# Rotating the second mixer and moving the column sums of the norms in a Trainium2 kernel of two transformer blocks

## Chip, cores and metric

The kernel runs on one core of one Trainium2 chip. The metric is the device time of one execution in microseconds (us); lower is better. A difference of about 0.2% is what a measurement of this kernel can tell from none.

## What is computed

Two transformer-like blocks in one launch, on a sequence of 512 tokens with width 1024, all in float32. Cut to what matters:

```python
# first block (depth 1)
x = x + 0.5 * swiglu(rmsnorm(x)) ;  x = x + mixer1(rmsnorm(x)) @ w_out ;  x = x + 0.5 * swiglu(rmsnorm(x))
# second block (depth 2): layer 0 has the even mixer, layer 1 the odd one
for layer in range(2):
    mix = even_or_odd_mixer(rms_norm(x, g[layer, 0]))
    x = x + rms_norm(mix, g[layer, 1])                 # a post-norm
    h = rms_norm(x, g[layer, 2])                       # a pre-norm
    x = x + rms_norm(conv_ffn(h), g[layer, 3])         # a post-norm

def even_mixer(h, w_in, w_out, w_sc, rel_bias):        # "the second mixer"
    gate_b, gate_c, xa, q, k, v = split(h @ w_in)      # six parts of 512 columns
    y_a = gate_b * causal_dwconv(gate_c * xa, w_sc)
    y_b = dilated_attention(q, k, v, rel_bias)         # 8 heads of 64
    return concat([y_a, y_b]) @ w_out
```

## The kernel before

**Layout.** Activations stand transposed, features on the 128 partitions and the 512 tokens in a row. `xT` holds the residual stream as 8 tiles of 128x512. A product that must be float32-exact enough is made of three passes on TensorE: every weight and every activation is split into a high part of type fp32r and the remainder (`wH`, `wL`, `H`, `L`), and `products` (L1853 on, its matmuls at L1860, L1861, L1862) adds H·wH, L·wH and H·wL. A **unit** is one 128-column slice of a weight matrix: 24 matmuls for 8 input tiles, or 33 for 11.

**Streams.** A `Stream` is one weight matrix. SyncE's queue loads a unit into a `raw` buffer (`load_unit`, L1842), ScalarE makes `wH` (`split_hi`, L1848), VectorE `wL` (`split_lo`, L1853), then TensorE multiplies. `wH`/`wL` are a ring of four slots, so a unit's split waits for the product that last used its slot. `st.bank` says which of the eight PSUM banks a unit is summed in.

**Order.** Every engine's instruction order is written out by hand; engines meet only at semaphores. The phases are: FFN 1, mixer 1, FFN 2, mixer 2 (stream IN2), its output projection (OUT2), conv-FFN 3 (GU3, DN3), mixer 3 (IN3, OUT3), conv-FFN 4 (GU4, DN4).

**Entry of a phase behind a post-norm** (there are three: `gu3`, `in3`, `gu4`; functions `proj_act`, `proj_dve`, `proj_pe`, `enter_act`, `enter_dve`, `first_products`, `ffn_pe`). The last tile of the projection is squared by ScalarE (L1909), VectorE adds it to the running sum `ssq` (L1917), and TensorE multiplies `ssq` with a matrix of 1/1024 (`column_sum`, L1889), which gives the mean on all partitions. ScalarE's `root` (L1922 Ln, L1924 Exp) makes `rstd`. Then for each of eight tiles VectorE scales (L1976), adds to `xT` (L1979) and makes the low part (L1934), and ScalarE makes the high part (L1929). In the same loop ScalarE squares the new tile (L1951) and VectorE adds it (L1970), for the pre-norm that follows. TensorE begins with `first_products`: for each tile as it becomes ready, its three matmuls for each of the first four units, 96 in all. After the seventh tile (`stat_after=6`) it makes the column sum of the pre-norm. The norm's factor is applied when the products are read from PSUM (L2097 in an FFN, L1331 in mixer 3), since it is per token.

**A conv-FFN** then goes, for each of its 22 feature tiles: gate product times `rstd` (VectorE L2097), convolution (ScalarE L2044, VectorE L2108 twice), Silu (L2048), times the up product (L2117), high part (L2052), low part (L2121). The splits of later units stand between these in the order of both engines.

**Mixer 2** (`conv_attention_mixer`) has four bodies p = 0 to 3, each with six units, in the order gate_b, gate_c, xa, q, k, v (j = 0 to 5), and two heads. Body p multiplies the units of p+1 and lets the attention of p run between them: scores (L971, `bank4`, `bank5`), softmax on VectorE and ScalarE, transposes of the probabilities (`pe_probT`, L981, all in `bank6`), their copy to SBUF (`act_probT`, L770), products with v (`pe_pv_pair`, L999, `bank7`). There are eight transposes s = 0 to 7 for each p, even s for one head and odd s for the other. The last body has no units left; there the first five of eight input tiles of the four first OUT2 units (`proj_start`, 15 matmuls each) stand between. Weights of body p+1 that share `bank0`, `bank1` wait for ScalarE's `evac` of the earlier unit.

**Mixer 3** begins with `first_products`, and its queue on SyncE waits for all eight low parts (`u_ready`) before it loads the mask `before` and then units (1,0) and on (L1134 to L1138).

The lines that set the transposes' waits are:

```python
    def pe_probT(pe, p, s):
        pe.wait_ge(M.scaled, 8 * p + (s + 1))
        if s == 0:
            pe.wait_ge(M.v_ev, p + 1)
        else:
            pe.wait_ge(M.p_ev, 8 * p + s)          # the copy of transpose s-1
```

Of the kernel before, what the change touches and what calls it, by code (L numbers as in the profile page):

```python
# [68 lines left out]
class Stream:  # L69
# [5 lines left out]
    def __init__(self, dram, bodies, per, K, early=False, extra=None, split=None, first=None):  # L75
# [5 lines left out]
        self.bank = {4: (0, 1, 2, 3), 5: (0, 1, 2, 3, 0), 6: (0, 1, 2, 3, 0, 1), 7: (0, 1, 2, 3, 0, 1, 2)}[per]  # L81
# [605 lines left out]
def conv_attention_mixer(k, st, t, site):  # L687
# [9 lines left out]
    FIRST_BANK = (5, 6, 7, 0, 1, 2)  # L697
    k.free("m2", site.scratch)
# [41 lines left out]
    def evac(act, u, j):  # L740
# [6 lines left out]
        if j == 0:  # L747
            wait(act, M.yc, u)
            act.activation(gb[:], src, ACT.Copy).then_inc(M.evac, 1)
        elif j in (1, 2):  # L750
            wait(act, M.cu, u)
            act.activation((gc, xa)[j - 1][:], src, ACT.Copy).then_inc(M.evac, 1)
        elif j in (3, 4):
            wait(act, M.scores, 8 * u)
            act.activation(qk[:, j - 3], src, ACT.Copy, scale=0.125 if j == 3 else 1.0).then_inc(M.evac, 1)
        else:
            wait(act, M.v_tr, u)
            act.activation(vT[:], src, ACT.Copy).then_inc(M.evac, 1)
# [7 lines left out]
    def act_probT(act, p, s):  # L766
        w = score_tile(s // 2)
        act.wait_ge(M.p_tr, 8 * p + (s + 1))
        wait(act, M.pv, 8 * p + (s - 1))
        act.activation(probT[:, s % 2, 0:w], bank[6][:, 0:w], ACT.Copy).then_inc(M.p_ev, 1)  # L770

    def act(act, after):
        def body(p, units, prev, tail):
            u = p + 1

            def slot(j):
                if units and not (isinstance(u, int) and u == 0 and j < st.early):
                    k.split_hi(act, st, u, j)
                if prev and not units and j < after.early:
                    k.split_hi(act, after, 0, j)  # L780
# [6 lines left out]
            if prev:  # L787
                evac(act, p, 3)
                evac(act, p, 4)
            slot(1)  # L790
            if prev:
                evac(act, p, 5)
# [12 lines left out]
            if units:  # L805
                evac(act, u, 0)
            slot(3)
            if prev:
                act.wait_ge(M.yc, p + 1)
                act.activation(k.tile_of(k.H, site.y + p), yc[:], ACT.Copy).then_inc(M.yc_hi, 1)  # L810
                act.wait_ge(M.v_tr, p + 1)
                act.activation(v_tok[:], bank[6][:].rearrange("p (a n) -> p a n", a=4), ACT.Copy).then_inc(M.v_ev, 1)
            if units:
                evac(act, u, 1)
            slot(4)
            if prev:
                act_probT(act, p, 0)
                act_probs(act, p, 2)
                act_probT(act, p, 1)
                act_probs(act, p, 3)  # L820
            if units:
                evac(act, u, 2)
            slot(5)
            if prev:
                act_probT(act, p, 2)
                act_probs(act, p, 4)
                act_probT(act, p, 3)
                act_probs(act, p, 5)
        k.split_hi(act, st, 0, 4)
        k.normal_act(act, site, 0, 4)  # L830
        k.split_hi(act, st, 0, 5)
        k.normal_act(act, site, 4, DT)
        act.wait_ge(M.tab_sum, 2)
        act.dma_start(t["dist_table"], table[0:8, :]).then_inc(M.tab_out, 16)
        act.wait_ge(M.tab_out, 16)
        load_params(act, 0)
        body(0, True, True, False)
# [29 lines left out]
    def dve_scaled(dve, j):  # L867
# [3 lines left out]
        dst, src, by = (gb[:], gc[:], xa[:], qk[:, 0], qk[:, 1], vT[:])[j], bank[FIRST_BANK[j]][:], k.rstd_mix[:]  # L871
        if j == 3:
# [3 lines left out]

    def dve(dve, after):
        def body(p, units, prev, tail):
            u = p + 1

            def slot(j):
# [1818 lines left out]
```

## Time and profile before

| | us |
|---|---|
| median of three runs | 2425.26 (2423.40 to 2427.48) |
| the profiled execution, its own time | 2428.54 |
| its span, first to last instruction | 2425.7 |
| TensorE matmuls busy | 2360.0 (97%) |
| VectorE busy | 1293.6 (53%) |
| ScalarE busy | 995.1 (41%) |
| GpSimd busy | 159.0 (7%) |
| mean granted TensorE clock | 0.989 |

The profile follows one execution. "Idle before" a row is time in which that engine did nothing ahead of it, with the instruction whose semaphore ended the wait. In a timeline the first column is the start in us from the span's start, the second the duration of the merged instructions; the end of a matmul is modelled, so distances are best taken from start to start.

### The profile page before, as it was taken

To read this page: it belongs to the slowest core of one execution; us is meant where nothing else is said; L and a number is where in the kernel's file an instruction comes from. 1 tells how busy PE (TensorE), PEld (TensorE's weight loads), DVE (VectorE), ACT (ScalarE), POOL (GpSimd) and SP (SyncE) were. 2 spreads that over 40 slices of the span, in tenths; PEclk is the share of its full clock that TensorE was granted. 3 is DMA by queue.
4 is the path that set the end of the run, shared out by engine and by line. 5 is a ranking of instruction groups with operands and counts; after the bars stand their busy time and mean duration, and the time that the engine had idled before them with its cause. 6 is when DMAs were issued, how large, how long until landed. Compare 5 with 4: busy or idle time off the path is not lost.

```text
span 2425.7 us, 30921 instructions
## 1 busy us (share of the span) xinstructions
PE 2360.0 (97%) x10918; PEld 1900.0 (78%) x10918; DVE 1293.6 (53%) x1832; ACT 995.1 (41%) x1481; POOL 159.0 (7%) x140
## 2 busy tenths in 40 slices
PE   8999999999999899999999989999989998999998
PEld 6888887777777688888877678888877766888887
DVE  5444436666655634433465475554258986655524
ACT  4222225756677422232234444333234454433322
POOL 0000002334333000000000000000000000000000
PEclk9999999999999999999999999999999998999999
DMA  4332322222322222232222122323213212232321
GB/s 163 97 99 100 106 91 93 83 100 73 99 73 84 79 94 95 95 106 96 93 90 96 61 71 94 101 91 120 95 35 106 77 63 70 81 101 95 118 96 47
DMA packets 62183, 219.91 MB, mean 91 GB/s; under 512 B 7664, under 2 KB 12272, under 8 KB 62112
## 3 DMA queue, kind: packets, MB, share of 16 engines
q1 hardware_dynamic: 60944, 216.86, 27.0%
q10 hardware_dynamic: 1168, 2.12, 0.3%
q8 instruction: 43, 0.70, 0.1%
q14 instruction: 28, 0.23, 0.0%
HBM read 216.83 MB, written 2.12 MB: 90 GB/s over the span
## 4 chain that ended last, share of the span: by engine, by line
PE 86%; DVE 5%; ACT 5%; issue 3%; DMA 0%; ACTq 0%; DVEq 0%; SPq 0%
PE bank L1860 26%; PE bank L1861 26%; PE bank L1862 26%; ACT m_prob L239 1%; DVE wL L1853 1%; PE bank L549 1%; ACT wH L1848 1%; DVE m_prob L358 1%; PE bank L592 0%; PE bank L971 0%; PE bank L999 0%; PE bank L981 0%; DVE m_mx L363 0%; PE bank L1559 0%; PE bank L2232 0%
## 5 line engine op out<-in xcount | busy, mean ns | idle before, releaser
L1860 PE MATMUL bank<-H,wH 128*128 128x512 f32 x3012 | 1194.4, 397 | 33.4 <-DVE L L1934 15.4
L1861 PE MATMUL bank<-L,wH 128*128 128x512 f32 x3012 | 1177.8, 391 | 0.0
L1862 PE MATMUL bank<-H,wL 128*128 128x512 f32 x3012 | 1177.8, 391 | 0.0
L1853 DVE TENSOR_TENSOR wL<-raw,wH 128x1024 fp32r<-128x1024 f32 (+1 forms) x361 | 470.9, 1311 | 611.9 <-ACT wH L1848 611.8
L1860 PEld LDWEIGHTS bank<-H,wH 128*128 128x128 f32 x3012 | 568.6, 189 | 166.2 <-issue 22.9
L1862 PEld LDWEIGHTS bank<-H,wL 128*128 128x128 f32 x3012 | 568.8, 189 | 120.6
L1861 PEld LDWEIGHTS bank<-L,wH 128*128 128x128 f32 x3012 | 569.2, 189 | 118.4 <-issue 3.8
L1848 ACT ACTIVATE wH<-raw 128x1024 fp32r<-128x1024 f32 (+1 forms) x361 | 396.5, 1106 | 213.2 <-PE bank L1862 204.6
L2052 ACT ACTIVATE H<-prod 128x512 f32 (+1 forms) x88 | 55.7, 633 | 243.5 <-DVE prod L2117 243.5
L2097 DVE TENSOR_TENSOR gate_s<-bank,rstd 128x512 f32<-128x512 f32 x88 | 60.8, 691 | 113.9 <-PE bank L1862 111.8
L2117 DVE TENSOR_TENSOR prod<-silu_g,bank 128x512 f32<-128x512 f32 x88 | 60.3, 685 | 79.7 <-PE bank L1862 73.6
L634 POOL TENSOR_TENSOR m_bias<-m_run,m_mask 128x256 f32<-128x256 f32 x64 | 77.2, 1244 | 382.8 <-DMA m_run<-in_rpb 382.8
L1929 ACT ACTIVATE H<-xT,cols 128x512 fp32r<-128x512 f32 (+1 forms) x56 | 39.9, 722 | 151.4 <-DVE xT L2379 120.6
L2041 ACT ACTIVATE silu_g<-gate_s 128x512 f32<-128x512 f32 x44 | 27.9, 633 | 162.0 <-DVE gate_s L2097 162.0
L2044 ACT ACTIVATE silu_g<-gate_s,cols 128x512 f32<-128x512 f32 x44 | 35.9, 815 | 114.5 <-DVE gate_s L2097 114.5
L2108 DVE SCALAR_TENSOR_TENSOR silu_g<-gate_s,cols,silu_g 128x511 f32<-128x511 f32 x88 | 66.1, 751 | 30.7 <-ACT silu_g L2044 25.1
L239 ACT ACTIVATE m_prob<-m_prob,m_mx 128x256 f32<-128x256 f32 x64 | 32.1, 502 | 72.5 <-DVE m_mx L363 72.5
L2121 DVE TENSOR_TENSOR L<-prod,H 128x512 f32 (+1 forms) x88 | 60.1, 683 | 3.0 <-ACT H L2052 2.8
L2048 ACT ACTIVATE silu_g<-silu_g 128x512 f32<-128x512 f32 x44 | 27.8, 632 | 76.8 <-DVE silu_g L2108 76.8
L1367 DVE SCALAR_TENSOR_TENSOR m_acc<-m_gp,cols,m_acc 128x512 f32<-128x512 f32 x84 | 57.5, 746 | 0.0
L1909 ACT ACTIVATE square<-mixT 128x512 f32<-128x512 f32 (+1 forms) x28 | 17.7, 632 | 96.8 <-DVE mixT L2370 51.2
L1934 DVE SCALAR_TENSOR_TENSOR L<-xT,cols,H 128x512 fp32r<-128x512 f32 (+1 forms) x56 | 41.2, 745 | 4.8 <-ACT H L1929 4.8
(267 smaller groups left out, 1670.6 us busy)
## 6 DMA issues: line engine op xcount, KB each, us to landing
raw<-in_w_ffn_gu SPq DMA_DIRECT2D x88, 512.0 KB, 3.4
raw<-in_w_in SPq DMA_DIRECT2D x56, 512.0 KB, 3.6
raw<-in_w_ffn_down SPq DMA_DIRECT2D x32, 704.0 KB, 4.1
raw<-in_w_up_2a SPq DMA_DIRECT2D x44, 512.0 KB, 3.4
raw<-in_w_up_2b SPq DMA_DIRECT2D x44, 512.0 KB, 3.4
raw<-in_w_in_even SPq DMA_DIRECT2D x24, 512.0 KB, 4.6
raw<-in_w_in_odd SPq DMA_DIRECT2D x24, 512.0 KB, 3.4
raw<-in_w_down_2a SPq DMA_DIRECT2D x16, 704.0 KB, 4.2
```

The source lines that it names most:

```text
L239: act.activation(prob[:, s % 2, 256 * b:256 * b + 256], prob[:, s % 2, 256 * b:256 * b + 256], ACT.Exp, bias=mx[:, e:e + 1], accum_out=den ...
L634: pool.tensor_tensor(bias[:, hh, n].rearrange("p (c r) -> p c r", r=ROWS), src, mask[:, MASK_OF[n]].rearrange("p (c r) -> p c r", r=ROWS), ...
L1367: dve.scalar_tensor_tensor(dst, src, w, dst, ALU.mult, ALU.add).then_inc(M.cv, 1)
L1848: act.activation(split_at(st, i, j)[0], raw_at(st, j), ACT.Copy).then_inc(S.hi_done, 1)
L1853: dve.tensor_tensor(w_l, raw_at(st, j), w_h.bitcast(F32), ALU.subtract).then_inc(S.lo_done, 1)
L1860: pe.matmul(out, w_h, xh[:, k0 + k], start=start and k == ks[0], stop=False)
L1861: pe.matmul(out, w_h, xl[:, k0 + k], start=False, stop=False)
L1862: last = pe.matmul(out, w_l, xh[:, k0 + k], start=False, stop=stop and k == ks[-1])
L2097: dve.tensor_tensor(gate_s[:, b], ffn_bank(i, 2 * b)[:], rstd[:], ALU.mult).then_inc(S.gate_ev, 1)
L2108: dve.scalar_tensor_tensor(silu_g[:, b, shift:], gate_s[:, b, 0:SEQ - shift], colr(w, (2 - shift) * FT + 2 * i + b), silu_g[:, b, shift:], ...
L2117: dve.tensor_tensor(prod[:, b], silu_g[:, b], ffn_bank(i, 2 * b + 1)[:], ALU.mult).then_inc(S.prod_done, 1)
L2121: dve.tensor_tensor(tile_of(L, ab + 2 * i + b), prod[:, b], tile_of(H, ab + 2 * i + b).bitcast(F32), ALU.subtract).then_inc(S.a_ready, 1)
```

## The change

It has three parts, which can be made one without the other.

1. **Mixer 2 is rotated.** The columns of its weights are reordered on the host to q, k, v, gate_b, gate_c, xa, and each body now multiplies gate_b, gate_c, xa of its own p and q, k, v of p+1. The last body therefore has three full units, and three of the four `proj_start` pieces; the fourth stands behind the last product with v. A piece covers six input tiles (18 matmuls). Units use three banks only, and the transposes of odd s go to `bank3`, so that a transpose waits for the copy of the one before the last. The convolution moves on VectorE behind scores 2 and 3. The table of distances is made right behind the first products.
2. **The last square of a post-norm** is no longer added by VectorE. TensorE multiplies `ssq` without it and the square itself into one bank (`post_sum`).
3. **The squares of the three pre-norms** stand behind all eight tiles and behind the splits of units (1,0) and (1,1). The column sum moves: in `gu3` and `gu4` behind unit (1,0), in `in3` behind the eighth tile.

```diff
+    T_BANK = (6, 3)
...
-        act.activation(probT[:, s % 2, 0:w], bank[6][:, 0:w], ACT.Copy).then_inc(M.p_ev, 1)
+        act.activation(probT[:, s % 2, 0:w], bank[T_BANK[s % 2]][:, 0:w], ACT.Copy).then_inc(M.p_ev, 1)
+
+    def unit_at(p, n):
+
+        return (p, n + 3) if n < 3 else (p + 1, n - 3)
...
-    early = (0, 1, 2, 4, 5)
+    early = (0, 1, 2, 4, 5, 6)
...
-        else:
-            pe.wait_ge(M.p_ev, 8 * p + s)
+        elif s > 1:
+            pe.wait_ge(M.p_ev, 8 * p + s - 1)
...
+        k.first_products(pe, c, site, [bank[b][:] for b in FIRST_BANK[:2]])
+        pe_table(pe)
+        dense(0, 2)
...
-    IN2 = Stream(t["w_in_even_2"], 4, 6, 8)
+    IN2 = Stream(t["w_in_even_2"], 4, 6, 8, banks=(0, 1, 2, 0, 1, 2))
...
-        gu3 = site(GU3, 0, 5, 32, gain(g2, 16), 4, 3, 6, rstd, post=gain(g2, 8), mix=0)
-        in3 = site(IN3, 0, 7, 40, gain(g2, 32), 4, 2, 6, rstd_mix, post=gain(g2, 24), mix=0, y=8,
-                   scratch=16)
-        gu4 = site(GU4, 22, 9, 48, gain(g2, 48), 4, 3, 6, rstd, post=gain(g2, 40), mix=22)
+        gu3 = site(GU3, 0, 5, 32, gain(g2, 16), 4, 3, None, rstd, post=gain(g2, 8), mix=0, squares_last=True)
+        in3 = site(IN3, 0, 7, 40, gain(g2, 32), 4, 2, 7, rstd_mix, post=gain(g2, 24), mix=0, y=8,
+                   scratch=16, squares_last=True)
+        gu4 = site(GU4, 22, 9, 48, gain(g2, 48), 4, 3, None, rstd, post=gain(g2, 40), mix=22, squares_last=True)
...
+        def post_sum(pe, c, on):
+
+            pe.wait_ge(S.ssq_done, adds(c.sums) + 7)
+            pe.matmul(bank[on][:], ones[:], ssq[:], start=True, stop=False)
+            c.sums += 1
+            pe.wait_ge(S.sq_done, 8 * c.sums)
+            pe.matmul(bank[on][:], ones[:], square[:, 1], start=False, stop=True).then_inc(S.stat_done, 1)
+            c.norms += 1
...
             for i, j in ((1, 0), (1, 1)):
                 split_hi(act, st, i, j)
+            for n in range(DT if site.squares_last else 0):
+                square2(n)
+            c.posts += 1
             root(act, c, site.stat_bank, site.rstd)
...
             for i, j in ((1, 0), (1, 1)):
                 split_lo(dve, st, i, j)
+            for n in range(1, DT if site.squares_last else 1):
+                add_square2(n)
+            c.posts += 1
...
                 unit_product(pe, st, 1, j, ffn_bank(1, j)[:], (H, L), site.u, True, True)
+                if j == 0 and site.squares_last:
+                    column_sum(pe, c, site.stat_bank, True)
...
-                add_square(dve, q, DT - 1, 1)
+                dve.wait_ge(S.sq_done, 8 * q + DT)
                 dve.tensor_copy(mixT[:, nxt.mix + DT - 1], bank[per - 1][:]).then_inc(S.proj_ev, 1)
```

Two places show the new order. The first is TensorE at the end of mixer 2's last body (`bank6`, `bank3` take transposed probabilities, `bank7` the products with v; the sizes are of the output). Before:

```order
L971 MATMUL bank4<-m2_qk_120 128x512 [waits m2_biased]
L971 MATMUL bank5<-m2_qk_120 128x512
L981 MATMUL bank6<-ident_58,m2_prob_122 128x128 [waits m2_p_ev,m2_scaled]
L981 MATMUL bank6<-ident_58,m2_prob_122 128x128 x2
L981 MATMUL bank6<-ident_58,m2_prob_122 128x128 [waits m2_p_ev,m2_scaled]
L981 MATMUL bank6<-ident_58,m2_prob_122 128x128 x3
L999 MATMUL bank7<-m2_probT_123,m2_v_tok_124 64x128 [waits m2_p_ev]
L999 MATMUL bank7<-m2_probT_123,m2_v_tok_124 64x128 x5
```

and in the change:

```order
L1871 MATMUL bank2<-H_50,wH_55 128x512
L1872 MATMUL bank2<-L_51,wH_55 128x512
L1873 MATMUL bank2<-H_50,wL_56 128x512
L990 MATMUL bank6<-ident_58,m2_prob_122 128x128 [waits m2_p_ev,m2_scaled]
L990 MATMUL bank6<-ident_58,m2_prob_122 128x128 x3
L1008 MATMUL bank7<-m2_probT_123,m2_v_tok_124 64x128 [waits m2_p_ev]
L1008 MATMUL bank7<-m2_probT_123,m2_v_tok_124 64x128 x5
L990 MATMUL bank3<-ident_58,m2_prob_122 128x128 [waits m2_p_ev,m2_scaled]
```

Before, transpose 6 follows transpose 5 and the last scores with nothing between; now 18 matmuls of an OUT2 unit stand ahead of it, and transpose 7 goes to another bank.

The second is VectorE in the entry `gu3`, from the last two tiles to the first gate. Before:

```order
L1976 SCALAR_TENSOR_TENSOR hf<-mixT,cols,rstd 128x512
L1979 TENSOR_TENSOR xT<-xT,hf 128x512
L1934 SCALAR_TENSOR_TENSOR L<-xT,cols,H 128x512
L1970 TENSOR_TENSOR ssq<-ssq,square 128x512
L1934 SCALAR_TENSOR_TENSOR L<-xT,cols,H 128x512
L1970 TENSOR_TENSOR ssq<-ssq,square 128x512
L1853 TENSOR_TENSOR wL<-raw,wH 128x1024 x2
L2097 TENSOR_TENSOR gate_s<-bank,rstd 128x512
```

and in the change:

```order
L2006 SCALAR_TENSOR_TENSOR hf<-mixT,cols,rstd 128x512
L2009 TENSOR_TENSOR xT<-xT,hf 128x512
L1958 SCALAR_TENSOR_TENSOR L<-xT,cols,H 128x512 x2
L1864 TENSOR_TENSOR wL<-raw,wH 128x1024 x2
L2000 TENSOR_TENSOR ssq<-square 128x512
L2000 TENSOR_TENSOR ssq<-ssq,square 128x512 x6
L2131 TENSOR_TENSOR gate_s<-bank,rstd 128x512
```

All seven additions of squares now stand between the splits and the first gate.

## Rows read from the trace of the kernel before

**Rows 1.** The page's first part: busy time, share and instructions of each engine.
```profile
PE 2360.0 (97%) x10918; PEld 1900.0 (78%) x10918; DVE 1293.6 (53%) x1832; ACT 995.1 (41%) x1481; POOL 159.0 (7%) x140
```
**Rows 2.** Waits of TensorE: who waited for whom, total us, times, longest us.
```profile
PE bank L1860 <- DVE L L1934: 15.4, 3, 5.2
...
PE bank L1889 <- DVE ssq L1917: 5.0, 3, 2.2
PE bank L981 <- ACT m_probT L770: 3.6, 4, 1.0
...
PE bank L981 <- DVE m_prob L864: 2.2, 1, 2.2
...
PE bank L999 <- ACT m_probT L770: 1.4, 2, 0.7
```
**Rows 3.** Timeline of TensorE in mixer 2: transposes and the last product with v.
```profile
1277.78 0.63 PE L981 MATMUL bank<-ident,m_prob 128*128 128x128 f32 x4 [0.97 <-ACT m_probT L770]
...
1388.95 0.97 PE L981 MATMUL bank<-ident,m_prob 128*128 128x128 f32 x4 [2.24 <-DVE m_prob L864]
...
1394.01 1.98 PE L999 MATMUL bank<-m_probT,m_v_tok 128*64 128x128 f32 x16 [0.69 <-ACT m_probT L770]
```
**Rows 4.** Busy time by stretch in mixer 2's last bodies; the column PEclk is the granted clock.
```profile
1362.00:1367.00 5.00, 3.48 (x41) 2.56 (x39) 4.20 (x7) 2.74 (x4) 0.00 (x0) 1.00 0.61 193
...
1392.00:1396.00 4.00, 3.08 (x21) 2.38 (x21) 0.00 (x0) 0.68 (x2) 0.00 (x0) 0.50 0.00 0
1396.00:1399.50 3.50, 3.50 (x9) 2.77 (x10) 1.39 (x2) 1.91 (x2) 0.00 (x0) 0.52 0.02 5
```
**Rows 5.** Timelines of VectorE and TensorE where OUT2's first units end.
```profile
1401.95 0.69 DVE L2372 COPY mixT<-bank 128x512 f32<-128x512 f32 x1 [1.37 <-PE bank L1862]
...
1404.29 1.23 DVE L1853 TENSOR_TENSOR wL<-raw,wH 128x1024 fp32r<-128x1024 f32 x1 [1.31 <-ACT wH L1848]
...
1405.83 0.40 PE L1860 MATMUL bank<-H,wH 128*128 128x512 f32 x1
```
**Rows 6.** Timelines of ScalarE and VectorE at the post-norm ahead of `gu3`.
```profile
1428.33 1.99 ACT L1848 ACTIVATE extraH<-raw 128x1024 fp32r<-128x1024 f32 x2
1430.38 0.69 ACT L1922 ACTIVATE rs<-bank,eps_col 128x512 f32<-128x512 f32 x1
...
1428.47 0.69 DVE L1917 TENSOR_TENSOR ssq<-ssq,square 128x512 f32<-128x512 f32 x1 [1.90 <-ACT square L1909]
...
1429.68 2.35 DVE L1853 TENSOR_TENSOR extraL<-raw,extraH 128x1024 fp32r<-128x1024 f32 x2
```
**Rows 7.** Timelines of TensorE and VectorE from `gu3`'s column sum to unit (2,1).
```profile
1456.99 1.02 PE L1889 MATMUL bank<-ssq,ones 128*128 128x512 f32 x2
1457.45 0.80 PE L1860 MATMUL bank<-H,wH 128*128 128x512 f32 x1
...
1459.44 0.69 DVE L2097 TENSOR_TENSOR gate_s<-bank,rstd 128x512 f32<-128x512 f32 x1 [4.51 <-PE bank L1862]
...
1465.59 1.23 DVE L1853 TENSOR_TENSOR wL<-raw,wH 128x1024 fp32r<-128x1024 f32 x1 [0.26 <-ACT wH L1848]
...
1484.95 1.23 DVE L1853 TENSOR_TENSOR wL<-raw,wH 128x1024 fp32r<-128x1024 f32 x1 [1.65 <-ACT wH L1848]
...
1487.82 0.39 PE L1860 MATMUL bank<-H,wH 128*128 128x512 f32 x1
```
**Rows 8.** Timelines of VectorE, SyncE's queue, ScalarE and TensorE in the entry `in3`.
```profile
1819.50 0.74 DVE L1976 SCALAR_TENSOR_TENSOR hf<-mixT,cols,rstd 128x512 f32<-128x512 f32 x1
...
1822.15 0.75 DVE L1934 SCALAR_TENSOR_TENSOR L<-xT,cols,H 128x512 fp32r<-128x512 f32 x1
1822.81 0.69 DVE L1970 TENSOR_TENSOR ssq<-ssq,square 128x512 f32<-128x512 f32 x1
...
1822.92 0.33 SPq L1135 DMA_DIRECT2D m_before<-in_before  x1
...
1827.41 2.26 ACT L1848 ACTIVATE wH<-raw 128x1024 fp32r<-128x1024 f32 x2 [5.17 <-DMA raw<-in_w_in_odd]
...
1828.80 0.80 PE L1860 MATMUL bank<-H,wH 128*128 128x512 f32 x1
```

More of the change, by code:

```diff
@@ L73, with __init__ @@
     newest = None
-    def __init__(self, dram, bodies, per, K, early=False, extra=None, split=None, first=None):
+    def __init__(self, dram, bodies, per, K, early=False, extra=None, split=None, first=None, banks=None):
         self.dram, self.bodies, self.per, self.K, self.extra = dram, bodies, per, K, extra
@@ L1007, in pe, with dense @@
     def pe(pe, c, after):
-        def body(p, units, prev, tail):
-            u = p + 1
-            def unit(j):
-                if not units:
-                    if prev and 1 <= j <= after.early:
-                        if j == 1:
-                            pe.wait_ge(M.evac, PER * N)
-                            for f in early:
-                                y_ready(pe)(f)
-                        k.proj_start(pe, after, j - 1, site.y, early)
+        def dense(i, j):
+            back = next(b for b in range(1, PER + 1) if st.bank[(j - b) % PER] == st.bank[j])
+            wait(pe, M.evac, PER * i + (j - back + 1))
+            if isinstance(i, int) and i == 0:
+                k.unit_product(pe, st, 0, j, bank[FIRST_BANK[j]][:], k.HL, site.u, True, True)
+            else:
+                k.unit_product(pe, st, i, j, bank[st.bank[j]][:], k.HL, site.v, True, True,
+                               v_ready(pe) if isinstance(i, int) and i == 1 and j == 0 else None)
@@ L1020, in unit @@
+        def body(p, units, prev, tail):
+            def unit(n):
+                if (n < 3 and prev) or (n >= 3 and units):
+                    dense(*unit_at(p, n))
                     return
-                if isinstance(u, int) and u == 0 and j < 2:
-                    if j == 0:
-                        k.first_products(pe, c, site, [bank[b][:] for b in FIRST_BANK[:2]])
+                if not (prev or n == 0):
                     return
-                back = next(b for b in range(1, PER + 1) if st.bank[(j - b) % PER] == st.bank[j])
@@ L1026, in unit @@
[L1026 to L1032 removed]
+                j = n - 3 if prev else 3
+                if j == 0:
+                    for f in early:
+                        y_ready(pe)(f)
@@ L1033, in body @@
+                if j < 3:
+                    pe.wait_ge(M.evac, PER * (N - 1) + (j + 4))
+                k.proj_start(pe, after, j, site.y, early)
+            if prev:
+                unit(0)
             if tail:
                 pe_pv_pair(pe, p - 1, 3)
+            if not prev:
+                unit(0)
             if prev:
```

230 lines of the change are left out of this document (112 added, 118 removed).

## The prediction

> **What bounds the kernel.** I read the busy shares first: TensorE is busy 97% of the span [rows 1], so only its idle time and its slow stretches can be won. The list of its waits says where that idle time is [rows 2]. Three kinds touch the change. At the three post-norms it waits 5.0 us for the last addition of squares, and then 15.4 us for the first low part of the new tiles. In mixer 2 it waits 3.6 + 1.4 us for copies of transposed probabilities and once 2.2 us for a scaled one, 7.2 us in all. The timeline puts the longest of these in the last body, where transpose 6 has nothing ahead of it [rows 3], and the stretches show what it brings: the granted clock is 0.50 from 1392 to 1396 and 0.52 until 1399.5, the lower of its two levels (1.2 of 2.4 GHz), whereas a similar stretch of transposes and small products 30 us earlier has 1.00 [rows 4]. All other terms are slack: how long before TensorE wants a unit its low part is there.
>
> **Scale.** From 1457.45 to 1487.82 TensorE starts 132 matmuls in a row [rows 7]: 12 of the last tile of the first products and five units of 24. One of them follows a column sum and takes 0.41 us longer, so a matmul is 0.227 us and a unit 5.45 us. The column sum costs 0.87 us (0.46 until the next matmul starts, and those 0.41).
>
> **Part 1, mixer 2.** All products stay; only waits go.
> - In the loop transpose 7 waited 0.97 us for the copy of transpose 6 [rows 3]. It now needs the copy of transpose 5, made one unit earlier: that wait goes in each body.
> - The last body had pieces of 15 matmuls and nothing at the sixth place. Now there are three full units and three pieces of 18 (4.1 us). In the rows of before, scaled probabilities 6 were ready 2.7 us after the last scores, so the 2.24 us wait [rows 3] is covered. Of the 7.2 us one wait of 0.69 us stays: the copy of transpose 7 ahead of the last product with v [rows 3].
> - Without the 2.24 us gap I expect the clock to stay up. What the low clock costs: half of 3.08 busy us in 1392 to 1396, 0.48 of the 3.5 us behind it [rows 4], and some 1.0 us for transpose 6 and its products before 1392 (the transpose took 0.97 us, its like in the loop 0.63 [rows 3]): 4.2 us.
> - A new wait: OUT2's first units are finished with two input tiles each instead of three, six matmuls fewer in units (0,2) and (0,3), 1.4 us. Behind the end of (0,1) come copy, square, high and low part of (1,0) in a chain that ends 3.57 us later (1401.95 to 1405.52) and was 0.3 us early for 1405.83 [rows 5]. TensorE now waits 1.1 us.
> - VectorE's queue has changed too: the convolution (3.6 us) stands ahead of a split and scores 4. By the durations of before, scaled probabilities 4 come 1.3 us before TensorE wants them in the loop and 0.3 us before in the last body. No wait, but thin.
>
> Sum: 7.2 + 4.2 - 0.7 - 1.1 = **9.6 us gained**.
>
> **Part 2, the last square.** TensorE no longer waits for a 0.69 us addition; its extra matmul on `ssq` runs while ScalarE squares. But ScalarE has two high parts to make, until 1430.32, before the Ln at 1430.38 [rows 6], so the root comes only 0.1 us earlier. VectorE makes two low parts until 1432.03 [rows 6] before it scales a tile; its copy starts 0.6 us earlier, but the first low part waits for the first high part (1429.38), so it gains 0.26 us. In `in3` its low parts already waited for the high ones: 0.1 us. Worth **0.6 us**, contained in the next terms.
>
> **Part 3, `gu3` and `gu4`.** Is the square in the tile loop on the path? VectorE needs 2.65 us a tile (1819.50 to 1822.15 [rows 8], the same in all three), TensorE 12 x 0.227 = 2.72 us, and its first tile runs at the low clock. So the loop already keeps up, and a faster VectorE starts nothing earlier. What moves is the column sum. Before, it starts at 1456.99 and the first gate at 1459.44 [rows 7], 2.45 us later. Now the first products end at 1460.6 - 0.87 - 0.26 = 1459.5, unit (1,0) at 1464.9, and the sum starts there: 7.9 us later. The first gate moves as much, and with it the chain gate, convolution, Silu, product, high part, split, in which each engine waits for the other and neither for TensorE. The low part of (1,2), done at 1466.82 [rows 7], is now done at 1474.7, and TensorE wants it at 1459.5 + 10.9 + 0.9 = 1471.2: a stall of 3.5 us. The slack is smallest at unit (2,1): low part 1486.18, wanted at 1487.82 [rows 7]. It is done at 1494.1 now: TensorE is **6.3 us late, in each of the two**. After that the steady loop is slower on TensorE than the chain, so the loss neither grows nor comes back.
>
> And the clock? A gap of 2.24 us once brought the low clock, and nine matmuls then filled 3.5 us [rows 3, 4], so the 3.5 us stall may do so too: some twelve matmuls of unit (1,2) 0.2 us longer each, 2.4 us. I add nothing for it, because the units behind wait for the chain: unit (2,0) then ends at 1493.5, still before 1494.1. The Trainium skill (TensorE: Matmul & The Clock Gate, section "HAM oscillation — how this bites in real kernels") warns that TensorE falls back to half rate in a long wait and starts the next burst cold; the rows agree that it does, and counted on top of the stalls, as that section counts it, it would make the sum 4.9 + 2 x 2.4 = +9.7 us.
>
> **Part 3, `in3`.** Without six additions of 0.6 us ahead of it the last low part is ready 3.6 us earlier, at 1819.3, so SyncE's queue, which waits for it (1822.92), issues its loads earlier and the high parts that waited 5.17 us for them start at 1823.8 instead of 1827.41 [rows 8] and end at 1826.1. The low parts end at 1827.3. Now the seven additions: the second waits for a square (1.35 us), five more follow at 0.72 us: 1832.9. TensorE ends the eighth tile at 1831.0, waits 1.9 us and makes the sum: unit (1,0) starts at 1833.8 instead of 1828.80 + 0.41 + 2.73 = 1831.9. **1.9 us lost.** `rstd_mix` comes 4.6 us later, but the low parts for the units behind have over 5 us of slack. The load that this hangs on is the uncertain one; between a load that lands as late as before (5.5 us lost) and additions hidden (0.9 gained) I take the moved landing.
>
> **Sum.** -9.6 + 6.3 + 6.3 + 1.9 = +4.9 us. The profiled execution took 2428.54 us, 3.3 above the median; from its own time this gives 2433.4, from the median 2425.26 **2430.2 us**, 0.2% more. A measurement of this kernel tells about 0.2% from no change (4.85 us), so the forecast is "slightly slower" and stands on the bound.
>
> **Rivals.**
> - *The late root is absorbed, and the kernel is faster.* For: VectorE is only 53% busy [rows 1], and the chain may close up where it had idle time. Against: the idle time ahead of the splits at 1465.59 and 1484.95 ends with ScalarE's high part [rows 7], which is in the chain itself. It decides if the chain can make up more than 7.9 - 1.6 = 6.3 us before unit (2,1). Then -9.6 + 1.9, and part 2's 0.6: 2417.
> - *The rotated body has its own waits.* The 1.3 us margin of scaled probabilities 4 is worked out from before; if splits bound to the unit just finished push it over, each body loses 1 to 2 us, or the tail keeps its low clock (4.2 us). Half the gain: 2435. Against: the 1.00 over a like stretch [rows 4].
> - *The clock adds to the stalls.* If the low clock lasts past unit (2,0) in `gu3` and `gu4`: 2 x 2.4 us more, 2435. For: a gap of 2.24 us was enough once [rows 3, 4].
> - *The chain is partly absorbed*, 3 us late instead of 6.3: 2424.
>
> **How the numbers follow.** The forecast gets 0.52, with its own range 2426 to 2434, half above the bound and half below. The absorbed root gets 0.17 (faster), the mixer's own waits 0.17 and the clock 0.08 (slower), the partly absorbed chain 0.06 (same). Slower 0.26 + 0.17 + 0.08 = 0.51, same 0.26 + 0.06 = 0.32, faster 0.17. The range takes in the first two rivals with the load's bound: 2416 to 2438.
>
> **What would show it.** In the profile after: new waits of TensorE for `wL` in units (1,2) and (2,1) of `gu3` and `gu4`, about 6.3 us in each; the first gate 7.9 us later behind the first products; in `in3` a wait for `ssq` of about 2 us at the column sum; in mixer 2 no wait ahead of transpose 7, one wait of 0.7 us at its end, the clock at 1.00 there, and about 1 us ahead of OUT2's unit (1,0); no wait of 1.4 us ahead of the sums at the post-norms, but still some 5 us behind each. Wrong, if TensorE has no wait for `wL` in the FFN entries, or if mixer 2 keeps its waits.

## The result: 7.3 us slower, and where the time went

The change takes 2433.66 us (median of 8 runs, 2431.60 to 2436.89), the kernel before 2426.37 us (8 runs beside them): ratio 1.0031, interval 1.0022 to 1.0040. That is slower by more than the 0.2% that a measurement tells, and inside the forecast range. The profiled execution took 2436.6 us, with a span of 2434.8 us (before 2425.7) and a mean granted clock of 0.987 (0.989). Two executions in the experiments took several times as long as all others of their kernels, 9371.79 us with the early loads alone and 7203.28 us with the filled gap, and are left out of the medians below.

The busy shares are what they were [rows 1]:

```profile
PE 2366.3 (97%) x10924; PEld 1900.7 (78%) x10924; DVE 1292.7 (53%) x1829; ACT 995.6 (41%) x1481; POOL 159.3 (7%) x140
```

The six matmuls more are those of the three `post_sum`, two records each. The waits of TensorE tell the story [rows 2]:

```profile
PE bank L1871 <- DVE wL L1864: 21.6, 10, 9.0
PE bank L1871 <- DVE L L1958: 17.0, 3, 5.7
PE bank L1913 <- DVE ssq L2000: 3.5, 1, 3.5
...
PE bank L1008 <- ACT m_probT L771: 0.7, 1, 0.7
PE bank L1902 <- ACT square L1933: 0.6, 1, 0.6
PE bank L990 <- DVE m_prob L871: 0.2, 1, 0.2
```

The 5.0 us for the last addition have become 0.6 us for a square, but the three waits for the first low part behind them have grown from 15.4 to 17.0 us. Of the 7.2 us in mixer 2 are left 0.7 + 0.2. New are 3.5 us for `ssq` and, from mixer 2 on, seven waits for `wL` of 9.7 us together. The kernel before has waits for `wL` too, but all of them ahead of mixer 2 (11.9 us, and 11.9 there in the change):

```profile
PE bank L1860 <- DVE wL L1853: 11.9, 4, 9.2
```

The spans compare like this (us, from the timelines of TensorE). The first row begins with IN2's column sum, each other row with the last product of the projection before it, so the wait for a post-norm's sum counts to the row behind it, and part 2 is contained in these rows:

| stretch | before | after | difference | forecast |
|---|---|---|---|---|
| IN2's sum to OUT2's last product (mixer 2) | 222.3 | 212.7 | -9.6 | -9.6 |
| to DN3's last product (`gu3`) | 370.3 | 377.3 | +7.0 | +6.3 |
| to OUT3's last product (`in3`, mixer 3) | 244.1 | 248.85 | +4.75 | +1.9 |
| to DN4's last product (`gu4`) | 364.1 | 370.4 | +6.3 | +6.3 |
| the end | | | +0.7 | 0 |

The sum, +9.1, is the difference of the two spans.

**Mixer 2.** TensorE at the last transpose and at the start of OUT2's unit (1,0), and the stretches that answer to [rows 4]:

```profile
1382.91 0.66 PE L990 MATMUL bank<-ident,m_prob 128*128 128x128 f32 x4
1384.26 1.09 PE L1008 MATMUL bank<-m_probT,m_v_tok 128*64 128x128 f32 x16 [0.69 <-ACT m_probT L771]
...
1396.12 0.47 PE L1871 MATMUL bank<-H,wH 128*128 128x512 f32 x1 [1.03 <-DVE wL L1864]
```

```profile
1392.00:1396.00 4.00, 3.09 (x14) 2.24 (x12) 2.28 (x4) 1.99 (x3) 0.00 (x0) 1.00 0.00 0
1396.00:1399.50 3.50, 3.38 (x15) 2.81 (x16) 2.45 (x4) 1.58 (x2) 0.00 (x0) 1.00 0.45 150
```

The kept wait of 0.69 us, the new one of 1.03 us ahead of (1,0), and a granted clock of 1.00 throughout: each as forecast.

**`gu3`.** TensorE from the column sum, then VectorE's first gate and the two splits that TensorE waits for [rows 7]:

```profile
1455.83 1.02 PE L1913 MATMUL bank<-ssq,ones 128*128 128x512 f32 x2
...
1461.95 0.39 PE L1873 MATMUL bank<-H,wL 128*128 128x512 f32 x1
1465.70 0.65 PE L1871 MATMUL bank<-H,wH 128*128 128x512 f32 x1 [3.36 <-DVE wL L1864]
1466.14 0.63 PE L1872 MATMUL bank<-L,wH 128*128 128x512 f32 x1
...
1485.05 0.50 PE L1871 MATMUL bank<-H,wH 128*128 128x512 f32 x1 [0.61 <-DVE wL L1864]
```

```profile
1458.28 0.69 DVE L2131 TENSOR_TENSOR gate_s<-bank,rstd 128x512 f32<-128x512 f32 x1 [10.96 <-ACT rstd L1948]
...
1464.42 1.23 DVE L1864 TENSOR_TENSOR wL<-raw,wH 128x1024 fp32r<-128x1024 f32 x1 [0.25 <-ACT wH L1859]
...
1483.77 1.23 DVE L1864 TENSOR_TENSOR wL<-raw,wH 128x1024 fp32r<-128x1024 f32 x1 [1.65 <-ACT wH L1859]
```

Counted from OUT2's last product, the sum has moved from 29.35 to 37.82 us, 8.5 us. The gate still comes 2.45 us behind it, and the low parts of (1,2) and (2,1) end 8.5 us later as well (39.2 to 47.6 and 58.5 to 67.0). The chain moves as one rigid piece. TensorE meets it at (1,2) with 3.36 us and at (2,1) with 0.61 us. Its slack can be read off: from the start of the sum to DN3's last product it is 340.9 us where TensorE does not meet the chain (before) and 339.4 where it does (after), so the slack was 1.5 us, and 8.5 - 1.5 = 7.0 us is what the stage lost. In `gu4` the sum moved by 7.8 us, and 7.8 - 1.5 = 6.3.

**`in3`.** VectorE, TensorE and SyncE's queue [rows 8]:

```profile
1822.20 2.60 DVE L1864 TENSOR_TENSOR wL<-raw,wH 128x1024 fp32r<-128x1024 f32 x2 [5.40 <-ACT wH L1859]
...
1826.11 4.67 DVE L2000 TENSOR_TENSOR ssq<-ssq,square 128x512 f32<-128x512 f32 x6 [0.70 <-ACT square L1974]
```

```profile
1826.96 0.39 PE L1873 MATMUL bank<-H,extraL 128*128 128x512 f32 x1
1830.83 1.83 PE L1913 MATMUL bank<-ssq,ones 128*128 128x512 f32 x2 [3.49 <-DVE ssq L2000]
1831.68 1.41 PE L1871 MATMUL bank<-H,wH 128*128 128x512 f32 x1
1832.89 0.63 PE L1872 MATMUL bank<-L,wH 128*128 128x512 f32 x1
```

```profile
1816.83 0.33 SPq L1146 DMA_DIRECT2D m_before<-in_before  x1
```

Counted from DN3's last product, the queue starts 3.5 us earlier (21.6 instead of 25.0 us behind it), as forecast. But the additions end 3.5 us behind the tile products, and behind that wait the two matmuls of the sum take 1.83 us instead of 1.02: the clock is low.

### The profile page after: what moved, and what is told of

It reads as the page before. It is cut to its first block, busy times and chain, and to the rows that moved or that the text cites. A ratio compares the mean times of both kernels' runs of the same rounds, so it can differ in the third digit from the quotient of the medians.

```text
span 2434.8 us, 30922 instructions
## 1 busy us (share of the span) xinstructions
PE 2366.3 (97%) x10924; PEld 1900.7 (78%) x10924; DVE 1292.7 (53%) x1829; ACT 995.6 (41%) x1481; POOL 159.3 (7%) x140
## 4 chain that ended last, share of the span: by engine, by line
PE 84%; DVE 7%; ACT 5%; issue 3%; DMA 0%; ACTq 0%; DVEq 0%; SPq 0%
PE bank L1871 26%; PE bank L1872 25%; PE bank L1873 25%; DVE wL L1864 1%; ACT wH L1859 1%; PE bank L549 1%; ACT m_prob L239 1%; DVE m_prob L358 1%; PE bank L592 0%; PE bank L1604 0%; PE bank L980 0%; PE bank L1008 0%; PE bank L1570 0%; PE bank L2266 0%; PE bank L2265 0%
## 5 line engine op out<-in xcount | busy, mean ns | idle before, releaser
L1871 PE MATMUL bank<-H,wH 128*128 128x512 f32 x3012 | 1196.7, 397 | 44.8 <-DVE wL L1864 21.6
```

The costliest lines, as they stand in the source:

```text
L1871: pe.matmul(out, w_h, xh[:, k0 + k], start=start and k == ks[0], stop=False)
```

## Experiments

All times are medians; each group ran beside its own runs of the kernel before. In these, the kernel before took 2427.57 us (12 runs, the first four), 2426.87 us (33 runs, the next four) and 2427.17 us (17 runs, the last four). It differs by 1.2 us from group to group, so a time set against one of another group is no surer than that.

### The parts alone

First part 1, and nothing else of the change:

```diff
-        gu3 = site(GU3, 0, 5, 32, gain(g2, 16), 4, 3, None, rstd, post=gain(g2, 8), mix=0, squares_last=True)
+        gu3 = site(GU3, 0, 5, 32, gain(g2, 16), 4, 3, 6, rstd, post=gain(g2, 8), mix=0)
...
-                post_sum(pe, c, 4)
+                column_sum(pe, c, 4, False)
...
```

> Part 1 alone. Theory (the three parts add up; mixer 2 gains 9.6 us by waits and low clock that go): 9.6 us under the kernel before, about 2416.8. In its trace mixer 2 has one wait of 0.7 us and one of 1.0 us ahead of OUT2's unit (1,0), and the granted clock stays at 1.00. Rival (what mixer 2 gains is partly given back in later stages, so the loss at the FFN entries is only the other side of it): under 5 us gained.

Measured: 2416.95 us, ratio 0.9955 (0.9942 to 0.9969). The mixer's 9.6 us are real and stand alone: the row of mixer 2 is 212.7 us here too.

Parts 1 and 2 (only the site lines go back):

> Parts 1 and 2, squares of the pre-norms in the tile loop as before. Theory: 0.6 us under part 1 alone (0.26 us at gu3 and gu4, 0.1 at in3), so 10.2 us under before, about 2416.2. A reader who prices part 2 by the addition it saves (3 x 0.7 us) expects 2.1 us under part 1 alone.

Measured: 2417.35 us, ratio 0.9947 (0.9934 to 0.9961). By these times part 2 can't be told from nothing. The five runs fall into two groups, 2411.39 and 2412.20 us at a mean granted clock of 0.995 and 2417.35 to 2417.96 us at 0.990, so the median of 2417.35 us, from which later expectations start, is that of the upper group. The traces do show part 2. In the waits it takes 4.4 us from the sums and gives 1.6 us back at the first low part, because that part was not waiting for the sum alone. What is left is the distance from OUT2's last product to the first product behind the post-norm, before and in the change:

```profile
1427.41 0.39 PE L1862 MATMUL bank<-H,wL 128*128 128x512 f32 x1
...
1435.52 0.80 PE L1860 MATMUL bank<-H,wH 128*128 128x512 f32 x1 [5.18 <-DVE L L1934]
```

```profile
1417.78 0.40 PE L1873 MATMUL bank<-H,wL 128*128 128x512 f32 x1
...
1425.64 0.80 PE L1871 MATMUL bank<-H,wH 128*128 128x512 f32 x1 [5.65 <-DVE L L1958]
```

It is 8.11 and 7.86 us; at `in3` it is 8.69 and 8.62, at `gu4` 8.12 and 7.87. That is 0.25 + 0.07 + 0.25 us, as expected. But at the kernel's end the wait for the last sum is 1.8 us in every version with part 2 and 1.4 us in every one without it, so 0.35 us go back there.

Part 3 on the kernel before (mixer 2 and the last square as before):

> Part 3 alone on the kernel before. Theory: +6.3 us in each of gu3 and gu4, and 4 to 4.7 us in in3 (as the trace of the change shows it): 16.6 to 17.5 us over before, about 2443.4. Rival (the loss needs the shorter mixer 2): 8 us or less over.

Measured: 2441.13 us, ratio 1.0055 (1.0041 to 1.0068), 13.6 us more, not 16.6. By stretches `gu3` is +6.5, `gu4` +6.0, but `in3` with mixer 3 only +1.3. Its wait for the squares is 2.38 us there instead of 3.49, because 12 slow matmuls ahead of it (7 in the change) made the tile products end later, and mixer 3 itself had fewer slow matmuls than in the profile of before. So what `in3` costs depends on where the clock is low. The same shows in mixer 2, which this version leaves as it was: with a gap of 2.25 us at the same place its row is 221.0 us instead of 222.3.

### Where the sum stands in the FFNs

The change with `stat_after=6` in `gu3` and `gu4`, squares still behind the tiles:

```diff
-        gu3 = site(GU3, 0, 5, 32, gain(g2, 16), 4, 3, None, rstd, post=gain(g2, 8), mix=0, squares_last=True)
+        gu3 = site(GU3, 0, 5, 32, gain(g2, 16), 4, 3, 6, rstd, post=gain(g2, 8), mix=0, squares_last=True)
...
-                if j == 0 and site.squares_last:
-                    column_sum(pe, c, site.stat_bank, True)
```

> The change, but gu3 and gu4 make the column sum after the seventh tile again (stat_after=6); the squares stay behind the tiles and the splits. Theory (the place of the sum on TensorE is what costs, since the additions end at about the time the seventh tile is multiplied): 12 us under the change, about 2421.7, with a wait for ssq of under 0.5 us at the sum. Rival (the late squares on VectorE and ScalarE cost, wherever the sum stands): no more than 3 us under the change.

Measured: 2421.66 us, ratio 0.9977 (0.9966 to 0.9987): the 12 us come back. Its waits of TensorE:

```profile
PE bank L1871 <- DVE wL L1864: 13.1, 4, 9.2
PE bank L1913 <- DVE ssq L2000: 5.1, 2, 4.1
```

All stalls at (1,2) and (2,1) are gone: from mixer 2 on, only the wait of 1.03 us ahead of OUT2's (1,0) is left. Of the waits for `ssq`, 4.1 us are `in3`'s, and 0.92 us stand ahead of the sum of `gu4`, more than the 0.5 us expected; in `gu3`, where 13 matmuls were slow behind the post-norm and not 6, there is none. The stage `gu3` takes 370.6 us from sum to sum, with the squares in the loop (parts 1 and 2) 369.8, and that difference of 0.8 is four slow matmuls (13 against 9). In `gu4` it is 364.3 against 364.0 us, with four slow matmuls fewer (6 against 10), which make up for most of the wait of 0.92 us. So taking the squares out of the tile loop brought nothing, and nearly all of the cost was the late sum. One tile later:

```diff
-        gu3 = site(GU3, 0, 5, 32, gain(g2, 16), 4, 3, 6, rstd, post=gain(g2, 8), mix=0, squares_last=True)
+        gu3 = site(GU3, 0, 5, 32, gain(g2, 16), 4, 3, 7, rstd, post=gain(g2, 8), mix=0, squares_last=True)
...
```

> The change, but with the column sum of gu3 and gu4 behind the eighth tile's products instead of behind the first unit's high products (before: behind the seventh). Theory (the lateness of the sum is what costs, and only what exceeds the slack of the chain of low parts): the sum stands one tile later than in the version with seven tiles, some 2.5 us later than before and 5 us earlier than in the change, so of the 3.4 us stall at (1,2) at most 0.8 us is left in each stage: 0 to 1.6 us over the version with seven tiles (2421.7), 2422 to 2423.5. Rival (it is the square behind the tiles, not the place of the sum, that costs): the sum itself then waits for the squares, and the time stays within 2 us of the change, 2432 to 2435.

Measured: 2423.36 us, ratio 0.9990 (0.9981 to 0.9999). One wait of 0.6 us in each of the two stages, at (2,1): `gu3` +1.3 us and `gu4` +0.8 over the version with seven tiles. In `gu3` the sum stands 2.7 us later than with seven tiles, so 1.5 us were slack, the same as above. The slack of the chain ends where the forecast put it.

### The entry of mixer 3

`in3` as before in the otherwise unchanged change:

```diff
-        in3 = site(IN3, 0, 7, 40, gain(g2, 32), 4, 2, 7, rstd_mix, post=gain(g2, 24), mix=0, y=8,
-                   scratch=16, squares_last=True)
+        in3 = site(IN3, 0, 7, 40, gain(g2, 32), 4, 2, 6, rstd_mix, post=gain(g2, 24), mix=0, y=8,
+                   scratch=16)
```

> The change, but the post-norm of in3 as before: squares among the tiles, sum behind the seventh tile. Theory (the sum of in3 waits for its additions, 3.5 us, and its clock falls behind that wait): the stage takes back the 4.75 us that it lost, 2433.7 - 4.7 = 2429.0 us, range 2428 to 2430. Rival (what the trace shows lost in in3 is shifted from the stages beside it and comes back there as another wait): 2432 to 2434.

Measured: 2428.42 us, ratio 1.0014 (1.0005 to 1.0023), 5.2 under the change by medians and 4.1 by the ratios (expected 4.7). The stretch takes 244.1 us instead of 248.85.

Or the loads earlier, with the squares behind the tiles:

```diff
+        for j in range(2):
+            k.load_unit(sp, st, 1, j)
         sp.wait_ge(S.u_ready, site.u0 + DT)
         sp.dma_start(before[:], t["before"]).then_inc(M.mask_loaded, 16)
...
```

> The change, but SyncE issues in3's first two loads of the second unit before it waits for the scaled tiles of the stage, so that the units' high parts on ScalarE are not held and the squares behind them come earlier. Theory (the squares of in3 stand behind a high part that waited for its load, which is why the additions end 3.5 us behind the tiles' products): the wait for the squares goes or falls under 0.5 us, and with it the slow stretch: 2433.7 - 4.5 = 2429.2 us, range 2428 to 2431. Rival (the additions are set by their own pace of 0.80 us a tile behind the last tile, not by the load): the wait stays over 3 us and the time stays at 2433 to 2434.5.

Measured: 2427.54 us, ratio 1.0010 (1.0001 to 1.0019), 6.1 under the change by medians and 5.1 by the ratios. VectorE and TensorE of this version:

```profile
1817.99 4.67 DVE L2004 TENSOR_TENSOR ssq<-ssq,square 128x512 f32<-128x512 f32 x6 [0.70 <-ACT square L1978]
```

```profile
1825.14 0.40 PE L1877 MATMUL bank<-H,extraL 128*128 128x512 f32 x1
1825.37 1.02 PE L1917 MATMUL bank<-ssq,ones 128*128 128x512 f32 x2
```

The additions take the same 4.67 us, but they end 2.7 us ahead of the sum: no wait, no slow matmul behind it. What cost `in3` its time was the load. The stretch from DN3's last product up to the sum of `m_ln_sum` in mixer 3 is 4.5 us shorter than in the change, as expected; another 2.5 us come behind it, where the change's profile has slow matmuls and this one has none, and that was not forecast.

The same version shows what the clock does to a stall. At `gu3`'s (1,2) it waits as long as the change, but stays fast behind it:

```profile
1463.03 0.50 PE L1875 MATMUL bank<-H,wH 128*128 128x512 f32 x1 [3.36 <-DVE wL L1868]
1463.36 0.40 PE L1876 MATMUL bank<-L,wH 128*128 128x512 f32 x1
...
1476.01 0.50 PE L1875 MATMUL bank<-H,wH 128*128 128x512 f32 x1 [1.47 <-DVE wL L1868]
```

The change had 7 slow matmuls there (some 1.4 us) and then no wait at the next unit; here there are none, and 1.47 us of wait come instead. Both reach (2,1) with 0.6 us to wait, and unit (2,1) starts 29.2 us behind the sum in both. Four profiles have the sum of `gu3` behind unit (1,0), with 0, 7, 13 and 13 slow matmuls behind the stall (this version, the change, part 3 alone, `in3` as before); from the sum to DN3's last product they take 339.46, 339.44, 339.47 and 339.43 us. Behind this rigid chain the low clock costs nothing.

### What in mixer 2 brings the gain

Parts 1 and 2, but all transposes in one bank:

```diff
-    T_BANK = (6, 3)
+    T_BANK = (6, 6)
...
-        elif s > 1:
-            pe.wait_ge(M.p_ev, 8 * p + s - 1)
+        else:
+            pe.wait_ge(M.p_ev, 8 * p + s)
```

> The change's second mixer and its last square by TensorE, squares of the post-norms as before (2417.35), but the transposes of both heads in one bank, with the wait for the other head's copy as before. Theory (the bank takes away the waits ahead of the second head's transposes, some 1 us each in three of the bodies, while the new order fills what waits elsewhere): 2417.35 + 3 = 2420.3 us, range 2419 to 2422. Rival A (the new order alone, not the bank, brings the gain of 9.6 us): within 1 us of 2417.35. Rival B (the bank is all of it, order nothing): 2424 to 2427.

Measured: 2422.63 us, ratio 0.9984 (0.9975 to 0.9993): 5.3 over parts 1 and 2, outside what each theory expected. Its row of waits, and one of them:

```profile
PE bank L990 <- ACT m_probT L771: 6.4, 8, 1.1
```

```profile
1305.17 0.63 PE L990 MATMUL bank<-ident,m_prob 128*128 128x128 f32 x4 [0.83 <-ACT m_probT L771]
```

There are two waits in each of four bodies, not one in three: ahead of transpose 7 (0.83 us) in all, ahead of transpose 1 (0.66 us) in the first three and of transpose 5 (1.13 us) in the last. The kernel before has the same pair of scores ahead of transposes 1 and 5 and no wait there. What is new is on ScalarE: a high part stands ahead of the copy. In the first body, with TensorE's transposes around it:

```profile
1236.65 0.27 PE L990 MATMUL bank<-ident,m_prob 128*128 128x128 f32 x1
...
1238.22 0.30 PE L990 MATMUL bank<-ident,m_prob 128*128 128x128 f32 x1 [0.66 <-ACT m_probT L771]
```

```profile
1236.85 1.06 ACT L1859 ACTIVATE wH<-raw 128x1024 fp32r<-128x1024 f32 x1 [4.36 <-PE bank L1873]
1237.81 0.26 ACT L771 ACTIVATE m_probT<-bank 128x128 f32<-128x128 f32 x1
```

Mixer 2 is 7.4 us longer than with two banks (6.4 of them are these waits, the other 1.0 us stays open) and 2.2 us shorter than before. So of the 9.6 us the order without the bank brings 2.2, the bank on top 7.4. The old order with a second bank was not run, so what the bank alone would bring there is not shown; the waits for copies ahead of a transpose that it could take away are 3.6 us [rows 2].

Five tiles in the pieces instead of six:

```diff
-    early = (0, 1, 2, 4, 5, 6)
+    early = (0, 1, 2, 4, 5)
...
-    return Names(sp=sp, act=act, dve=dve, pe=pe, pool=pool, y_ready=y_ready, late=(3, 7))
+    return Names(sp=sp, act=act, dve=dve, pe=pe, pool=pool, y_ready=y_ready, late=(3, 6, 7))
```

> The change's second mixer and its last square by TensorE, squares of the post-norms as before (2417.35), but OUT2's pieces cover five input tiles as before instead of six, so that the units (0,2) and (0,3) are again finished with three tiles. Theory (the chain copy, square, high part, low part of unit (1,0) runs beside the end of those two units, and six matmuls fewer there, 1.4 us, left it 1.03 us late): the wait of 1.03 us ahead of unit (1,0) goes; the pieces are 0.68 us shorter, so a wait of up to 0.5 us for scaled probabilities may come in the last body. 2417.35 - 0.6 = 2416.7 us, range 2415.8 to 2417.4. Rival (the last body needs pieces of 18 matmuls to cover its softmax): waits of over 1 us in the last body, 2418 or more.

Measured: 2415.76 us, ratio 0.9961 (0.9948 to 0.9974), which is at the edge of the expected range and yet no support for the theory. The wait ahead of (1,0) is gone, but the last body has new ones; TensorE, and VectorE ahead of it:

```profile
1373.39 0.55 PE L990 MATMUL bank<-ident,m_prob 128*128 128x128 f32 x3 [1.58 <-DVE m_prob L871]
```

```profile
1369.45 0.69 DVE L896 TENSOR_TENSOR m_yc<-m_cc,m_gb 128x512 f32<-128x512 f32 x1
1370.06 1.22 DVE L1864 TENSOR_TENSOR wL<-raw,wH 128x1024 fp32r<-128x1024 f32 x1
...
1372.91 0.42 DVE L871 TENSOR_SCALAR m_prob<-m_prob,m_den 128x384 f32<-128x384 f32 x1
```

This is the place that the forecast called thin: convolution and split stand ahead of scores 4. With 18 matmuls a piece the wait is 0.22 us; two pieces shorter by 0.68 us make it 1.58, and another 0.37 us wait comes behind. Mixer 2 takes 213.4 us instead of 212.7. The rival's wait came; its time, 2418 us or more, did not. That the median is still lower than that of parts 1 and 2 fits the mean clock, 0.991 to 0.993 in these runs and 0.990 in those behind the 2417.35 us.

The kernel before, with its gap filled by repeated work (`repeated` makes the fourth piece's 15 matmuls into `bank3`, which `proj_start` then makes anew):

```diff
-                        k.proj_start(pe, after, j - 1, site.y, early)
+                        if j < 4:
+                            k.proj_start(pe, after, j - 1, site.y, early)
+                        else:
+                            repeated(after)
...
             unit(5)
+            if prev and not units:
+                k.proj_start(pe, after, 3, site.y, early)
```

> The kernel before, with 15 matmuls of 512 columns of repeated work (the fourth piece of OUT2's first units, made twice, the first time to no use) in the last body of mixer 2 where TensorE waits 2.24 us for scaled probabilities 6. Theory (that gap brings the low clock, which costs 4.2 us more): 15 x 0.227 = 3.4 us of work added, 2.24 us of wait gone, 4.2 us of low clock gone: 3.0 us under the kernel before, 2424, with the granted clock at 1.00 from 1392 to 1399.5 on. Rival (the low clock there is hidden or comes from elsewhere): 1.2 us over the kernel before, 2428.

Measured: 2422.71 us (ten runs), ratio 0.9986 (0.9977 to 0.9995): 15 useless matmuls made the kernel 4.5 us faster by medians, 3.4 by the ratio. The stretches:

```profile
1392.00:1396.00 4.00, 2.48 (x31) 1.86 (x28) 0.15 (x1) 1.19 (x2) 0.00 (x0) 1.00 0.02 4
1396.00:1399.50 3.50, 2.87 (x13) 2.01 (x13) 1.75 (x3) 1.92 (x2) 0.00 (x0) 1.00 0.00 0
```

The clock is 1.00 where it was 0.50 [rows 4]. Mixer 2 is 2.0 us shorter: 3.4 added, 2.24 of wait gone, a new wait of 0.63 us for a low part, so the low clock had cost 3.8 us (forecast 4.2). The median gained more than those 2.0 us. In the profiles the clock elsewhere does it: this one has no slow matmul in mixer 3, that of before has 12.

### A better version?

Parts 1 and 2 with the early loads, and with `in3` alone of part 3:

```diff
-        in3 = site(IN3, 0, 7, 40, gain(g2, 32), 4, 2, 6, rstd_mix, post=gain(g2, 24), mix=0, y=8,
-                   scratch=16)
+        in3 = site(IN3, 0, 7, 40, gain(g2, 32), 4, 2, 7, rstd_mix, post=gain(g2, 24), mix=0, y=8,
+                   scratch=16, squares_last=True)
...
+        for j in range(2):
+            k.load_unit(sp, st, 1, j)
...
```

> The change's second mixer and last square, gu3 and gu4 as before, and in3 with the squares behind the tiles and the first two loads of the second unit ahead of SyncE's wait. Theory (squares behind the tiles help where the sum does not have to wait for them: in the version of the change with early loads, in3 and its projection took 241.9 us from sum to sum, with squares in the loop 244.0): 2.1 us under 2417.35: 2415.3 us, range 2414.3 to 2416.3. Rival (those 2.1 us came from where the clock fell, not from in3): 2417 to 2418.

Measured: 2413.43 us, ratio 0.9953 (0.9940 to 0.9966), under the expected range. And without any of part 3:

> As the last one, but the squares of in3 in the tile loop as before; of the change's third part nothing is left, only the two early loads are added. Theory (no wait of TensorE in in3 hangs on these loads while the squares are in the loop): 2417.35 us within 0.7. Rival (the early loads, not the place of the squares, bring the 2.1 us): 2415.3 us within 0.7.

Measured: 2416.07 us (five runs), ratio 0.9959 (0.9946 to 0.9973), between what the two expected. Its trace decides for the theory: the row of `in3` is 243.96 us, with parts 1 and 2 alone 243.97, so the early loads alone bring nothing. The medians favour the version with `in3`, the ratios parts 1 and 2 (0.9947), and the trace speaks for the rival that was named first, that the 2.1 us come from the clock. The entry, from DN3's last product to the sum of `m_ln_sum`, is only 0.3 us shorter (188.9 against 189.3 us). The rest lies in mixer 3, behind one and the same wait. Parts 1 and 2, then the version with `in3`:

```profile
1994.53 0.79 PE L1871 MATMUL bank<-H,wH 128*128 128x512 f32 x1 [2.89 <-DVE L L1526]
1995.12 0.63 PE L1872 MATMUL bank<-L,wH 128*128 128x512 f32 x1
```

```profile
1993.17 0.50 PE L1875 MATMUL bank<-H,wH 128*128 128x512 f32 x1 [2.89 <-DVE L L1530]
1993.51 0.40 PE L1876 MATMUL bank<-L,wH 128*128 128x512 f32 x1
```

The granted clock of the 6 us behind is 0.55 in the one and 1.00 in the other; that is 1.8 us. At the same mean clock the three kernels are alike within 2.4 us: at 0.994 to 0.995 they take 2411.4 to 2413.7 us, at 0.990 2417.3 to 2419.6 us. So the versions without part 3 in the FFNs, all near 2413 to 2418 us, beat both kernels, and among them these runs choose none.

## Why the prediction was right, and where it was off

- **Mixer 2, 9.6 us: right, term by term.** Each of the waits, the clock and the 1.03 us ahead of (1,0) (forecast 1.1) are in the rows, and the part alone gives 10.6 us by medians. Inside the sum, the low clock was 3.8 us rather than 4.2, and the scaled probabilities 4 had 0.22 us of wait where I had 0.3 us of slack. With these the terms make 7.2 + 3.8 - 0.7 - 1.0 - 0.2 = 9.1 us; that the stretch shows just the forecast 9.6 is in part luck. The rival "the rotated body has its own waits" falls: these 0.2 us are its only wait, and the clock stayed at 1.00.
- **Part 2, 0.6 us: right where it was worked out** (0.25, 0.07 and 0.25 us at the three post-norms). What was missed is the 0.35 us that it costs at the kernel's end.
- **`gu3` and `gu4`, 6.3 us each: mechanism and place right.** Measured 7.0 and 6.3. The column sum moved by 8.5 us in `gu3` instead of 7.9, since 13 matmuls at the low clock followed the post-norm instead of 10. The version with seven tiles gives the 12 us back, and the one with eight finds the slack, 1.5 us where the forecast had 1.6 at (2,1). `gu4` meets the 6.3 us with the right terms (7.8 - 1.5 for 7.9 - 1.6). The rivals "the late root is absorbed" and "partly absorbed" fall: at the gate and at both low parts the chain was late by the same 8.5 us, to 0.03 us.
- **The clock behind the stalls: rightly left out.** The Trainium skill (TensorE: Matmul & The Clock Gate, section "HAM oscillation — how this bites in real kernels") has TensorE start cold behind a wait and counts that on top. The trace of the change agrees on the first in `gu3` (7 slow matmuls behind 3.36 us), that of the version with early loads does not (none behind the same 3.36 us). Neither agrees on the second: with the slow matmuls the next unit waited 1.47 us less, and the stage took as long.
- **`in3`, 1.9 us: the mis-sized term, 4.75 measured.** The moved load was right (1816.83). Three things were off. The additions have a pitch of 0.80 us, not the 0.72 that I assumed (six in 4.67 us, the last 0.69 long), and end 0.5 us later behind DN3's last product than forecast. The tile products end 1.2 us earlier, as 7 matmuls were slow behind this post-norm and 13 in the profile I worked from. Together they turn 1.9 us of wait into about the 3.49 measured. And the low clock behind this wait, which I did not price, costs more than 1 us, for here no chain hides it: four matmuls take 0.43 us each instead of 0.23, and the sum and the product behind it about 1 us more. Of the 4.75 us, 4.1 lie ahead of the sum of `m_ln_sum`; the last 0.6 us, behind it, are not shown to come from the change.
- **The end, 0.7 us,** was not in the sum; 0.35 us of it is the wait ahead of the last sum (1.8 instead of 1.4 us) that comes with part 2; the rest stays open.

The sum in spans was +9.1 against a forecast of +4.9. The medians differ by 7.3 us. Sign and mechanisms held; the size was short mainly by `in3`.

## What to carry to other kernels

Before moving a statistic later, follow what is released by it, not what is ahead of it: here the sum fed a chain of six steps between two engines that had 1.5 us of slack and was moved by 8. Work that an engine does in a loop is worth moving only if the loop waits for that engine. And a small gap in a thin stretch of transposes may be dearer than it looks: filling it even with useless matmuls paid.

## What was not expected of the hardware

**One kernel's times follow where the clock is low.** In the 62 runs of the kernel before beside the experiments, those with a mean granted clock of 0.988 took 2428.3 to 2429.9 us (19 runs), those with 0.992 2422.2 to 2422.7 us (4 runs). The instructions are the same. Only one of these executions has a profile, so that the waits are the same too is read across the profiles of all versions: in each a wait of 5.0 to 5.7 us stands behind each post-norm, and 5 to 13 matmuls at the low clock follow it. The Trainium skill (TensorE: Matmul & The Clock Gate, section "What's actually happening") says that the number of cold matmuls at a kernel's start varies from run to run; these profiles agree, 5 to 13, and show it in mid-kernel. Versions that differ by 5 us or less can therefore be ranked only by stretches free of it: from `gu3`'s sum to DN3's last product it took 340.91 us in all nine profiles with that sum behind the seventh tile.

**A wait's length alone does not tell whether the clock falls.** The 2.24 us in mixer 2 were followed by a clock of 0.50 [rows 4] in before; 2.89 us in mixer 3 by slow matmuls in one version and not in another; 3.36 us in `gu3` likewise.

**Two engines that hand over a tile each way keep a pitch above either's work:** squares of 0.63 us on ScalarE and additions of 0.69 us on VectorE, with two buffers between them, run at 0.80 us a tile in `in3` of the change, and ScalarE waits a little for VectorE at each:

```profile
1827.63 0.63 ACT L1974 ACTIVATE square<-xT 128x512 f32<-128x512 f32 x1 [0.16 <-DVE ssq L2000]
1828.42 0.63 ACT L1974 ACTIVATE square<-xT 128x512 f32<-128x512 f32 x1 [0.17 <-DVE ssq L2000]
```
